# Latent attention: two heads at a time, block by block, with 64-row rotary score products

## The chip, the cores and the metric

One core of one Trainium2 chip runs the whole program. The metric is the device time of one execution in microseconds (us), taken as the median of several runs.

## The reference

Two transformer blocks, in 32-bit floats, on 512 tokens of width 1024. The first block has windowed attention, a short convolution and a mixture of 16 experts. The second block has two layers with feed-forward parts; its last mixer is the multi-head latent attention that the change touches. For each of its 8 heads:

```python
k = jnp.concatenate([k_nope, jnp.broadcast_to(k_pe[:, :, None, :], (B, S, N_HEADS_2, QK_ROPE))], axis=-1)
q = rope_tail(rmsnorm_2(q, q_head_norm), cos, sin)     # 128 plain dims + 64 rotary dims
k = rope_tail(rmsnorm_2(k, k_head_norm), cos, sin)
s = jnp.einsum('bhqd,bhkd->bhqk', q_blk, kt) * scale   # blocks of 128 queries
s = jnp.where(kpos[None, :] <= qpos[:, None], s, -jnp.inf)
p = jax.nn.softmax(s, axis=-1)
o = jnp.einsum('bhqk,bhkv->bhqv', p, vt)
```

So a score is a sum over 128 plain dimensions and 64 rotary ones, of which the rotary key is one for all heads before its scaling per head.

## The kernel before

All five engines run one hand-written program each; semaphores order them, and every engine works through its own list in order. SyncE (SP) loads weights through a ring of strips; ScalarE (ACT) and VectorE (DVE) split a strip into a high and a low part (helpers `hi` and `lo`), and TensorE (PE) makes three products of them (`three`, L1123 to L1125). This fills most of the time. The latent attention lies between the query projections and the output projection (`whole`, L1140).

**Layout.** `qn` and `kn` hold the 128 plain dimensions of queries and keys of each head on the 128 partitions. `qr` holds rotary queries, two heads to a tile: head 2i on partitions 0 to 63, head 2i+1 on 64 to 127. `kr` has one tile of 512 keys for each head; the scaled rotary key is written (`head_scale`, L2460) on that half of the partitions on which the head's queries lie. The other half is zero, from one memset on GpSimd (POOL) at L659, which waits until the memory is free (`h_lo` and `sq_done`); VectorE waits for it in front of the first `head_scale` (L2508).

**Units.** A unit u is one head h and one block b of 128 queries, h, b = divmod(u, 4): all four blocks of a head, then the next head. Being causal, block b has w = 128 (b + 1) keys. There are 32 units. For each, in this order:

- `scores(u)`, PE: a 32-bit product `qn` x `kn` (L1758), then one `qr` x `kr` over all 128 partitions (L1759), which adds to it, in one of four PSUM banks (`S2`, banks 6, 7, 1, 0). It counts up `scored`. For u >= 4 it waits until VectorE has taken unit u-4 out of the bank (`masked`).
- `soft_max(u)`, DVE: adds the causal mask and takes the maximum (L2536), and makes the bias (L2541).
- `soft(u)`, ACT: the exponential with its sum (L1087).
- `invert_sum`, `scale_probs`, DVE: reciprocal (L2032) and scaling (L2037) of unit u-1, behind `soft_max(u)` in VectorE's list.
- `turn_probs(u)`, PE: b + 1 transposes of 128x128 (L1780) into bank 2 or 3; it waits for the scaled probabilities and for ScalarE's copy of unit u-2 (`pt_act`).
- `turn_out(u)`, ACT: copies them into `pT2` (L1095).

When all four blocks of a head are turned, `values(h)`, PE, makes the value products (L1788); ScalarE (`head_out`, L1100) and VectorE (L2554) split the result into high and low parts.

**Order.** Turning runs three units behind the scores (LAG = 3). PE's list is

```python
for u in range(2, MH * NB + LAG + 1):
    if u < MH * NB:
        scores(u)
    if 0 <= u - LAG < MH * NB:
        turn_probs(u - LAG)
    if head_at(u - LAG - 1) is not None:
        values(head_at(u - LAG - 1))
```

where `head_at(u)` is the head whose last block is unit u, or None. ACT's list has `soft(u)`, then `turn_out(u - LAG)`, then `head_out` of the head that ended with unit u-LAG-2; DVE's list has `soft_max(u)`, then the reciprocal and scaling of unit u-1, then L2554 for the head that ended with unit u-LAG-3. One weight strip for the output projection is split meanwhile (`hi` at u = 8, `lo` at u = 11). The first two units' scores lie between the last four value projections (`values_of(1, i)`), whose results ScalarE copies out of banks 1, 3, 2 and 0 (`value_out`, L1036, semaphore `valued`); unit 2 goes into bank 1 and unit 3 into bank 0, so they wait for five and eight of these copies.

Of the kernel before, what the change touches and what calls it, by code (L numbers as in the profile page):

```python
# [28 lines left out]
P = 128  # L29
# [5 lines left out]
NB = T // P  # L35
# [5 lines left out]
MH, NOPE, ROPE = 8, 128, 64  # L41
# [85 lines left out]
def build(nc, A, out):  # L127
    st = ExitStack()
    with st:
# [113 lines left out]
        kr = place("kr", [P, MH, T], F32, G)  # L243
# [3 lines left out]
        qn = place("qn", [P, MH, T], F32, G + 50 * KB)  # L247
        qr = place("qr", [P, 4, T], F32, G + 66 * KB)
# [152 lines left out]
        def q_scale(h, b):  # L401

            c = 32 + 16 * (h // 4) + 4 * b + h % 4
            return qstat[:, c:c + 1]

        def head_at(u):

            return u // NB if 0 <= u < MH * NB and u % NB == NB - 1 else None

        def halves(n):  # L410

# [12 lines left out]
        S2 = (6, 7, 1, 0)  # L424
# [219 lines left out]
        @block.gpsimd  # L644
        def _(pool):
            pool.memset(ones[:, :], 1.0).then_inc(ones_set, 1)
            pool.memset(eps[:, :], EPS).then_inc(ones_set, 1)
            pool.wait_ge(mod_summed, 2)
            pool.memset(kZ[64:128, 0, :], 0.0).then_inc(cleared, 1)
            pool.memset(kZ[0:64, 1, :], 0.0).then_inc(cleared, 1)  # L650

            pool.wait_ge(strip_used, POOL)
            pool.memset(zero[:, :].bitcast(F32), 0.0).then_inc(cleared, 1)

            pool.wait_ge(select_loaded, 16)
            pool.tensor_copy(select_r[:, :, :], select[:, :, :]).then_inc(pool_made, 1)
            pool.wait_ge(h_lo, LO0[N2B])
            pool.wait_ge(sq_done, SQ0[N2B])
            pool.memset(kr[:, :, :], 0.0).then_inc(pool_made, 1)  # L659


        @block.scalar
        def _(act):
# [417 lines left out]


            def soft(u):
                h, b = divmod(u, NB)
                act.wait_ge(bias_ready, 32 + u + 1)
                p = prob2[:, u % 4, 0:(b + 1) * P]
                act.activation(p, p, ACT.Exp, bias=stat[:, 16 + u % 4:17 + u % 4], scale=q_scale(h, b),  # L1087
                               accum_out=stat[:, 20 + u % 4:21 + u % 4]).then_inc(exp_done, 1)

            def turn_out(u):  # L1090
                h, b = divmod(u, NB)
                act.wait_ge(p_turned, 32 + u + 1)
                if b == 0 and h >= 2:
                    act.wait_ge(pv_done, NB + h - 1)
                act.activation(pT2[h % 2][:, 0:b + 1, b * P:(b + 1) * P],  # L1095
                               pb[2 + u % 2][:, 0:(b + 1) * P].rearrange("p (k q) -> p k q", q=P), ACT.Copy).then_inc(pt_act, 1)
# [22 lines left out]
        def _(pe):  # L1119
# [625 lines left out]
                if s == 9:  # L1745
                    qsum_turn(0)
            def scores(u):
                h, b = divmod(u, NB)
                w = (b + 1) * P
                if u == 0:  # L1750
                    pe.wait_ge(out_taken, T_MOUT)
                    pe.wait_ge(hq_out, 2 * MH)
                    pe.wait_ge(rope_done, 10)
                if u in (2, 3):
                    pe.wait_ge(valued, 5 if u == 2 else 8)
                if u >= 4:
                    pe.wait_ge(masked, 32 + u - 3)
                pe.matmul(pb[S2[u % 4]][:, 0:w], qn[:, h, b * P:(b + 1) * P], kn[:, h, 0:w], start=True, stop=False)  # L1758
                pe.matmul(pb[S2[u % 4]][:, 0:w], qr[:, h // 2, b * P:(b + 1) * P], kr[:, h, 0:w], start=False, stop=True).then_inc(scored, 1)  # L1759

            head_sum(19)
            values_of(0, 0)
# [6 lines left out]
            values_of(1, 1)  # L1769
            scores(0)  # L1770
            values_of(1, 2)
            scores(1)
            values_of(1, 3)

            def turn_probs(u):
                h, b = divmod(u, NB)
                pe.wait_ge(p_ready, 32 + u + 1)
                pe.wait_ge(pt_act, 32 + u - 1)
                for k in range(b + 1):
                    mm = pe.transpose(pb[2 + u % 2][:, k * P:(k + 1) * P], prob2[:, u % 4, k * P:(k + 1) * P], tab("ident"))  # L1780
                mm.then_inc(p_turned, 1)

            def values(h):
                pe.wait_ge(pt_act, 32 + NB * h + NB)
                if h >= 2:
                    pe.wait_ge(att_lo, NB + h - 1)
                for k in range(NB):
                    mm = pe.matmul(pb[4 + h % 2][:, k * P:T], V2[:, k, h * P:(h + 1) * P], pT2[h % 2][:, k, k * P:T],  # L1788
                                   start=(k == 0), stop=(k == NB - 1))
                mm.then_inc(pv_done, 1)  # L1790

            for u in range(2, MH * NB + LAG + 1):
                if u < MH * NB:
                    scores(u)
                if 0 <= u - LAG < MH * NB:
                    turn_probs(u - LAG)
                if head_at(u - LAG - 1) is not None:
                    values(head_at(u - LAG - 1))
# [6 lines left out]
        def _(dve):  # L1805
# [228 lines left out]
            def scale_probs(v, p):  # L2034

                dve.wait_ge(inv_ready, v + 1)
                dve.tensor_scalar(p, p, stat[:, 24 + v % 4:25 + v % 4], None, ALU.mult).then_inc(p_ready, 1)  # L2037
# [451 lines left out]
            for s in range(12):  # L2489
                if s != 2:  # L2490
                    lo(M_Q + s + 2)
                dve.wait_ge(strip_used, M_Q + s + 1)
                ps = pb[bank(T_MQ + s)][:, :]
                if s in Q_ROPE:
                    dve.tensor_scalar(qr[:, Q_ROPE[s], :], ps, col("qh_rope"), None, ALU.mult).then_inc(out_taken, 1)
                else:
                    dve.tensor_copy(qn[:, Q_NOPE[s], :], ps).then_inc(out_taken, 1)
                if s == 2:
                    dve.wait_ge(hq_std, 1)
                    dve.reciprocal(head_rstd[:, :], head_std[:, :]).then_inc(hq_rstd, 1)  # L2500
                    dve.wait_ge(hq_rstd, 1)
                    dve.tensor_copy(head_hi[:, :], head_rstd[:, :]).then_inc(hq_rstd, 1)
                    dve.wait_ge(hq_rstd, 2)
                    dve.tensor_tensor(head_lo[:, :], head_rstd[:, :], head_hi[:, :], ALU.subtract).then_inc(hq_rstd, 1)
                    lo(M_Q + 4)
                if 3 <= s <= 6:
                    if s == 3:
                        dve.wait_ge(pool_made, 2)  # L2508
                        dve.wait_ge(gained, 2)
                        dve.wait_ge(keyed, 8)  # L2510
                        dve.wait_ge(rope_done, 6)
                    head_scale(2 * s - 6)
                    head_scale(2 * s - 5)
                if s == 7:
                    invert(NQL)
                if 8 <= s <= 11:
                    r = s - 7
                    rope_finish(qr[:, r - 1, :], pb[7 - r % 2][:, :], rope2[:, 1, :], rope2[:, 0, :], rope_tmp[:, :], 5 + r)
                if s == 10:
                    mean_squares(0)  # L2520
# [4 lines left out]


            def soft_max(u):
                h, b = divmod(u, NB)
                w = (b + 1) * P
                m2 = stat[:, 32 + u % 4:33 + u % 4]  # L2530
                dve.wait_ge(scored, 32 + u + 1)
                if u >= 4:
                    dve.wait_ge(p_turned, 32 + u - 3)
                else:
                    dve.wait_ge(mask_loaded, 16)
                dve.tensor_tensor_reduce(prob2[:, u % 4, 0:w], pb[S2[u % 4]][:, 0:w], cmask[:, T - w:T], 1.0, -3e38,  # L2536
                                         ALU.add, ALU.max, m2).then_inc(masked, 1)
                dve.wait_ge(masked, 32 + u + 1)
                if u in (0, 4 * NB):
                    dve.wait_ge(scale_ready, NB if u == 0 else 2 * NB)  # L2540
                dve.tensor_scalar(stat[:, 16 + u % 4:17 + u % 4], m2, q_scale(h, b), -1.0, ALU.mult, ALU.mult).then_inc(bias_ready, 1)  # L2541

            for u in range(MH * NB + LAG + 3):
                if u < MH * NB:
                    soft_max(u)
                if u == 11:
                    lo(M_OUT + 1)
                if 1 <= u <= MH * NB:
                    invert_sum(32 + u - 1)
                    scale_probs(32 + u - 1, prob2[:, (u - 1) % 4, 0:((u - 1) % NB + 1) * P])  # L2550
                if head_at(u - LAG - 3) is not None:
                    h = head_at(u - LAG - 3)
                    dve.wait_ge(att_hi, NB + h + 1)
                    dve.tensor_tensor(oL[:, h, :], pb[4 + h % 2][:, :], oH[:, h, :], ALU.subtract).then_inc(att_lo, 1)  # L2554
# [101 lines left out]
```

## Time and profile before

| what | value |
|---|---|
| median of 3 runs | 2512.27 us (2511.79 to 2514.25) |
| span of the profiled execution, first to last instruction | 2510.8 us |
| own time of that execution beyond its span | not shown; the median is 1.5 us above the span |
| PE busy, share of the span | 2478.2 us, 99% |
| DVE / ACT / POOL busy | 1155.5 / 742.0 / 8.0 us |
| L1759, rotary scores | 64 records, all between 2035 and 2096 us |
| mean granted clock of TensorE | 0.996 of full speed |

A product of 32-bit floats stands in the profile as two records, each with its own load of weights. A record of a matmul is longer than the time after which the next one can start, since it holds the way through the array as well, so starts are to be compared, not lengths; the chain of waits does that. Busy time of PE that comes from overlapping records is counted once.

### The profile page before, as it was taken

The numbers are of one execution on the slowest core, as the hardware profiler recorded it, in microseconds if no ns is written. First come the engines' busy times: TensorE is split into PE (matmuls) and PEld (weight loads), VectorE is DVE, ScalarE is ACT, GpSimd is POOL, SyncE is SP. The second block draws the span as 40 slices with busy tenths as digits, with TensorE's granted clock in tenths as the row PEclk, the third lists the DMA queues.
The fourth block names the chain that finished last, engine by engine and source line by source line (L and its number), as shares of the span: only waits on it lengthen the run. The fifth ranks groups of instructions, "written<-read, shape, count | busy, mean of one in ns | idle before, by whom it ended". The sixth has DMA issues, their size and how long they took to land.

```text
span 2510.8 us, 29196 instructions
## 1 busy us (share of the span) xinstructions
PE 2478.2 (99%) x10958; PEld 1783.1 (71%) x10958; DVE 1155.5 (46%) x1802; ACT 742.0 (30%) x1066; POOL 8.0 (0%) x11
## 2 busy tenths in 40 slices
PE   8999999999999999999999999999999999999999
PEld 4876733333336888888888888888887667888887
DVE  6785612222227544436444434444337665544422
ACT  4245210100114333224333223333224354333311
POOL 0000000000000000000000000000000000000000
PEclk9999999999999999999999999999999999999999
DMA  7530899999993323313232322233322211323332
GB/s 308 176 126 31 320 394 422 421 422 422 422 411 133 100 92 110 104 63 102 92 100 95 115 82 92 93 100 105 104 81 76 80 43 35 98 94 100 105 104 68
DMA packets 84644, 404.12 MB, mean 161 GB/s; under 512 B 9176, under 2 KB 9560, under 8 KB 60896
## 3 DMA queue, kind: packets, MB, share of 16 engines
q1 hardware_dynamic: 84576, 403.22, 43.7%
q8 instruction: 42, 0.69, 0.1%
q14 instruction: 26, 0.21, 0.0%
HBM read 401.08 MB, written 2.10 MB: 161 GB/s over the span
## 4 chain that ended last, share of the span: by engine, by line
PE 92%; DVE 3%; ACT 2%; issue 1%; DMA 1%; SPq 0%; ACTq 0%; DVEq 0%
PE pair L1123 23%; PE pair L1125 23%; PE pair L1124 23%; PE pair L1399 9%; PE pair L1424 4%; PE pair L1350 2%; PE pair L1650 1%; PE pair L1370 1%; PE pair L1788 1%; PE pair L1265 1%; PE pair L1758 1%; PE pair L1759 1%; PE pair L1371 1%; ACT wH L676 0%; DMA stage<-in_gate 0%
## 5 line engine op out<-in xcount | busy, mean ns | idle before, releaser
L1813 DVE TENSOR_TENSOR wL<-stage,wH 128x1024 fp32r<-128x1024 f32 (+3 forms) x301 | 388.9, 1292 | 771.1 <-ACT wH L676 770.7
L1123 PE MATMUL pair<-hH,wH 128*128 128x512 f32 x1672 | 658.4, 394 | 7.8 <-DVE hL L1858 2.4
L1125 PE MATMUL pair<-hH,wL 128*128 128x512 f32 x1672 | 652.0, 390 | 0.0
L1124 PE MATMUL pair<-hL,wH 128*128 128x512 f32 x1672 | 652.0, 390 | 0.0
L676 ACT ACTIVATE wH<-stage 128x1024 fp32r<-128x1024 f32 (+3 forms) x301 | 335.3, 1114 | 846.9 <-PE pair L1125 843.4
L1123 PEld LDWEIGHTS pair<-hH,wH 128*128 128x128 f32 x1672 | 314.6, 188 | 78.4 <-DVE hL L1858 4.1
L1124 PEld LDWEIGHTS pair<-hL,wH 128*128 128x128 f32 x1672 | 314.6, 188 | 67.1 <-issue 2.4
L1125 PEld LDWEIGHTS pair<-hH,wL 128*128 128x128 f32 x1672 | 314.6, 188 | 66.3
L1123 PE MATMUL pair<-gH,wH 128*128 128x512 f32 x704 | 273.9, 389 | 0.0
L1124 PE MATMUL pair<-gL,wH 128*128 128x512 f32 x704 | 273.9, 389 | 0.0
L1125 PE MATMUL pair<-gH,wL 128*128 128x512 f32 x704 | 273.9, 389 | 0.0
L1399 PE MATMUL pair<-ring,xsT 128*64 128x512 f32 x1008 | 223.9, 595 | 1.5 <-ACT xsT L903 1.5
L1399 PEld LDWEIGHTS pair<-ring,xsT 128*64 128x64 f32 x1008 | 71.2, 137 | 138.0 <-issue 136.3
L1124 PEld LDWEIGHTS pair<-gL,wH 128*128 128x128 f32 x704 | 132.1, 188 | 27.7
L1123 PEld LDWEIGHTS pair<-gH,wH 128*128 128x128 f32 x704 | 132.1, 188 | 27.5
L1125 PEld LDWEIGHTS pair<-gH,wL 128*128 128x128 f32 x704 | 132.1, 188 | 27.2
L2189 DVE SCALAR_TENSOR_TENSOR x<-pair,mod,x 128x512 f32<-128x512 f32 x64 | 45.5, 747 | 135.8 <-PE pair L1371 135.8
L716 ACT ACTIVATE sg<-hraw 128x512 f32<-128x512 f32 x88 | 55.7, 633 | 167.1 <-DVE hraw L2284 167.1
L1424 PE MATMUL pair<-ring,hidT 128*64 128x512 f32 x448 | 99.2, 595 | 0.0
L2293 DVE TENSOR_TENSOR gL<-gf,gH 128x512 f32 (+1 forms) x88 | 61.0, 693 | 78.7 <-ACT gH L719 78.7
L910 ACT ACTIVATE sil<-pair 128x512 f32<-128x512 f32 x16 | 8.7, 594 | 245.6 <-PE pair L1399 245.6
L719 ACT ACTIVATE gH<-gf 128x512 f32 (+1 forms) x88 | 55.7, 633 | 76.7 <-DVE gf L2290 76.7
(353 smaller groups left out, 2148.3 us busy)
## 6 DMA issues: line engine op xcount, KB each, us to landing
ring<-in_experts SPq DMA_DIRECT2D x182, 1024.0 KB, 21.0
stage<-in_gate SPq DMA_DIRECT2D x88, 512.0 KB, 3.6
stage<-in_up SPq DMA_DIRECT2D x88, 512.0 KB, 3.6
stage<-in_down SPq DMA_DIRECT2D x64, 704.0 KB, 4.0
adaw<-in_w_ada SPq DMA_DIRECT2D x32, 512.0 KB, 5.4
stage<-in_w_in SPq DMA_DIRECT2D x18, 512.0 KB, 3.9
ring<-in_experts SPq DMA_DIRECT2D x16, 512.0 KB, 11.6
stage<-in_mla_in SPq DMA_DIRECT2D x9, 512.0 KB, 3.6
```

Source lines behind the costliest of these rows:

```text
L676: act.activation(halves(n)[0], stage[:, n % STAGE, 0:width[n]], ACT.Copy).then_inc(strip_hi, 1)
L716: act.activation(sg[:, tile % 2, :], hraw[:, tile % 2, :], ACT.Silu).then_inc(silu_done, 1)
L719: act.activation(dst, gf[:, tile % 2, :], ACT.Copy).then_inc(g_hi, 1)
L1123: pe.matmul(ps, lh, rh, start=first, stop=False)
L1124: pe.matmul(ps, lh, rl, start=False, stop=False)
L1125: return pe.matmul(ps, ll, rh, start=False, stop=last)
L1350: mm = pe.matmul(pb[6 + half][:, :], pick[:, k, :], xt[:, k, half * 512:(half + 1) * 512], start=(k == 0), stop=(k == NB - 1))
L1399: mm = pe.matmul(pb[2 * g + half][64 * j:64 * j + 64, :], xsT[:, k, 64 * j:64 * j + 64], w[j][:, half * 512:(half + 1) * 512], start=(k == ...
L1424: mm = pe.matmul(pb[4 + half][64 * j:64 * j + 64, :], hidT[:, k, 64 * j:64 * j + 64], w[j][:, half * 512:(half + 1) * 512], start=(k == 0) ...
L1813: dve.tensor_tensor(low, stage[:, n % STAGE, 0:w], high, ALU.subtract).then_inc(strip_lo, 1)
L2189: dve.scalar_tensor_tensor(out=x[:, k, :], in0=pb[7 - k % 2][:, :], scalar=mod[:, 40 + k:41 + k], in1=x[:, k, :], op0=ALU.mult, op1=ALU.ad ...
L2293: dve.tensor_tensor(gL[:, g, :], gf[:, s, :], gH[:, g, :], ALU.subtract).then_inc(g_lo, 1)
```

## The change

- Units are renumbered: `head_block(u)` gives heads 2i and 2i+1 in turn, block by block: (head 0, block 0), (head 1, block 0), (head 0, block 1), and so on. `head_at` and all users of h and b follow, and so do the counts that `values` waits for.
- `scores(u)` runs for even u alone and makes both units: the two plain products, then the two rotary ones. The rotary product of head 2i reads partitions 0 to 63 of `qr` and `kr`, that of head 2i+1 partitions 64 to 127.
- It waits for `masked` of unit u-3 in place of u-4, and for u = 2 for all eight value copies. Unit 1's scores move to the place of unit 0's, ahead of the last two value projections.
- The memset of `kr` goes; VectorE waits for `h_lo` and `sq_done` itself.

```diff
+        def head_block(u):
+
+            two, rest = divmod(u, 2 * NB)
+            return 2 * two + rest % 2, rest // 2
+
         def head_at(u):
 
-            return u // NB if 0 <= u < MH * NB and u % NB == NB - 1 else None
+            return head_block(u)[0] if 0 <= u < MH * NB and head_block(u)[1] == NB - 1 else None
...
             pool.tensor_copy(select_r[:, :, :], select[:, :, :]).then_inc(pool_made, 1)
-            pool.wait_ge(h_lo, LO0[N2B])
-            pool.wait_ge(sq_done, SQ0[N2B])
-            pool.memset(kr[:, :, :], 0.0).then_inc(pool_made, 1)
...
             def soft(u):
-                h, b = divmod(u, NB)
+                h, b = head_block(u)
...
             def scores(u):
-                h, b = divmod(u, NB)
+
+                h, b = head_block(u)
                 w = (b + 1) * P
...
-                if u in (2, 3):
-                    pe.wait_ge(valued, 5 if u == 2 else 8)
+                if u == 2:
+                    pe.wait_ge(valued, 8)
                 if u >= 4:
-                    pe.wait_ge(masked, 32 + u - 3)
-                pe.matmul(pb[S2[u % 4]][:, 0:w], qn[:, h, b * P:(b + 1) * P], kn[:, h, 0:w], start=True, stop=False)
-                pe.matmul(pb[S2[u % 4]][:, 0:w], qr[:, h // 2, b * P:(b + 1) * P], kr[:, h, 0:w], start=False, stop=True).then_inc(scored, 1)
+                    pe.wait_ge(masked, 32 + u - 2)
+                for j in range(2):
+                    pe.matmul(pb[S2[(u + j) % 4]][:, 0:w], qn[:, h + j, b * P:(b + 1) * P], kn[:, h + j, 0:w], start=True, stop=False)
+                for j in range(2):
+                    rows = slice(64 * j, 64 * j + 64)
+                    pe.matmul(pb[S2[(u + j) % 4]][:, 0:w], qr[rows, h // 2, b * P:(b + 1) * P], kr[rows, h + j, 0:w],
+                              start=False, stop=True).then_inc(scored, 1)
...
             scores(0)
             values_of(1, 2)
-            scores(1)
             values_of(1, 3)
...
             def values(h):
-                pe.wait_ge(pt_act, 32 + NB * h + NB)
+                pe.wait_ge(pt_act, 32 + 2 * NB * (h // 2) + 2 * (NB - 1) + h % 2 + 1)
...
             for u in range(2, MH * NB + LAG + 1):
-                if u < MH * NB:
+                if u < MH * NB and u % 2 == 0:
                     scores(u)
...
                     if s == 3:
-                        dve.wait_ge(pool_made, 2)
+                        dve.wait_ge(h_lo, LO0[N2B])
+                        dve.wait_ge(sq_done, SQ0[N2B])
```

`turn_out`, `turn_probs`, `soft_max` and the scaling of unit u-1 take h and b from `head_block` in the same way. The lists of ACT and DVE keep their order by u.

## Rows read from the trace of the kernel before

**Rows 1.** Windows view, 2057 to 2103 us: length, busy time of each engine, PEclk, DMA.
```profile
core 0 of [0], span 2510.8 us
2057.00:2103.00 46.00, 45.05 (x196) 29.21 (x197) 28.96 (x112) 26.09 (x73) 0.00 (x0) 1.00 0.04 12
```

**Rows 2.** Chain of waits, one head's period: start us, length us, what.
```profile
2064.87 2.38 PE pair L1788 x8
...
2068.35 0.43 PE pair L1759 x2
2068.78 0.33 PE pair L1780 x3
...
2069.75 0.65 PE pair L1759 x2
...
2071.70 0.86 PE pair L1759 x2
...
2072.66 2.38 PE pair L1788 x8
```

**Rows 3.** Timeline of PE, first block's attention: start us, length us, what.
```profile
195.72 0.71 PE L1252 MATMUL pair<-tabs,prob 128*128 128x128 f32 x5
196.36 4.51 PE L1265 MATMUL pair<-PT,V 128*64 128x512 f32 x20
200.81 0.70 PE L1236 MATMUL pair<-kZ,qT 128*128 128x256 f32 x2
201.34 0.59 PE L1237 MATMUL pair<-kZ,qT 128*128 128x256 f32 x2
```

**Rows 4.** Timeline of PE, window means of the pool mixer, 1146.59 to 1148.58 us.
```profile
1146.59 0.49 PE L1590 MATMUL pair<-zero 1*128 1x512 f32 x1
1147.01 1.22 PE L1594 MATMUL pair<-band,tok 128*128 128x144 f32 x8
1148.16 0.49 PE L1590 MATMUL pair<-zero 1*128 1x512 f32 x1
```

**Rows 5.** Timeline of all engines behind a 512-key unit's scores, 2080.19 us on.
```profile
2080.19 0.27 PE L1780 MATMUL pair<-tabs,prob 128*128 128x128 f32 x1
2080.39 0.69 DVE L2536 CUSTOM_DVE_ANT_0 prob<-pair,cmask 128x512 f32<-128x512 f32 x1 [0.88 <-PE pair L1759]
...
2081.12 0.21 DVE L2541 TENSOR_SCALAR stat<-stat,qstat 128x1 f32<-128x1 f32 x1
...
2081.37 0.82 ACT L1087 ACTIVATE prob<-prob,stat,qstat 128x512 f32<-128x512 f32 x1 [1.01 <-DVE stat L2541]
...
2081.44 0.42 DVE L2037 TENSOR_SCALAR prob<-prob,stat 128x384 f32<-128x384 f32 x1
2082.09 0.18 ACT L1087 ACTIVATION_READ_ACCUMULATOR prob<-prob,stat,qstat 128x1 f32 x1
```

**Rows 6.** Groups by form, 2035 to 2103 us, ACT: busy us, mean ns, idle before.
```profile
L1095 ACT ACTIVATE pT2b<-pair 128x384 f32<-128x384 f32 x4 | 1.9, 484 | 0.0
...
L1036 ACT ACTIVATE V<-pair 128x512 f32<-128x512 f32 x3 | 1.8, 591 | 0.0
```

**Rows 7.** Timeline of PE at two of its waits, then the chain at the end.
```profile
2043.22 0.59 PE L1759 MATMUL pair<-kr,qr 128*128 128x256 f32 x2
2044.41 0.30 PE L1780 MATMUL pair<-tabs,prob 128*128 128x128 f32 x1 [0.59 <-ACT pT2a L1095]
...
2056.00 0.27 PE L1780 MATMUL pair<-tabs,prob 128*128 128x128 f32 x1
2057.03 0.70 PE L1788 MATMUL pair<-pT2b,V 128*128 128x512 f32 x1 [0.75 <-ACT pT2b L1095]
...
2096.05 2.38 PE pair L1788 x8
...
2100.53 2.42 PE pair L1788 x8
```

**Rows 8.** Source view of the memset of kr and of kr's first writer: durations, first start.
```profile
L659 POOL MEMSET kr<- x1: 3735/3735/3735, 1937.7 to 1937.7; 128x4096 f32 x1
...
L2460 DVE TENSOR_TENSOR kr<-krope,pair x8: 671/682/693, 1975.5 to 1996.2; 64x512 f32<-64x512 f32 x8
```

More of the change, by code:

```diff
@@ L1747, in scores @@
             def scores(u):
-                h, b = divmod(u, NB)
+                h, b = head_block(u)
                 w = (b + 1) * P
@@ L1771, in _ @@
             values_of(1, 2)
-            scores(1)
             values_of(1, 3)
             def turn_probs(u):
-                h, b = divmod(u, NB)
+                h, b = head_block(u)
                 pe.wait_ge(p_ready, 32 + u + 1)
@@ L2527, in soft_max @@
             def soft_max(u):
-                h, b = divmod(u, NB)
+                h, b = head_block(u)
                 w = (b + 1) * P
@@ L2549, in _ @@
                     invert_sum(32 + u - 1)
-                    scale_probs(32 + u - 1, prob2[:, (u - 1) % 4, 0:((u - 1) % NB + 1) * P])
+                    scale_probs(32 + u - 1, prob2[:, (u - 1) % 4, 0:(head_block(u - 1)[1] + 1) * P])
                 if head_at(u - LAG - 3) is not None:
```

## The prediction

> **What bounds the kernel now.** I read the granted clock and busy time of the stretch first. In the settled part of the latent attention, 2057 to 2103 us, the matmul side of TensorE is busy 45.05 of 46 us at full clock (PEclk 1.00, the 2.4 GHz level), and VectorE and ScalarE 29 and 26 us [rows 1]. So TensorE sets the pace and the others have idle time, on the average of the stretch. Then the chain of waits for one head, from one value product to the next: 2064.87 to 2072.66, 7.79 us [rows 2]. It is TensorE all the way: the score products without rotary (L1758), those with it (L1759), the turning of the probabilities (L1780), the value product (L1788). The two score products cost the same at each width, 0.43, 0.65 and 0.86 us for 256, 384 and 512 keys (0.22 for 128, a quarter of the last), though half of the partitions of the rotary one hold zeros. Below, S(u), T(u) and V(h) are the scores, the turning and the values of unit u and head h, C(u) ScalarE's copy of T(u), and w the width.
>
> **Term 1, the rotary products.** Per head L1759 takes 0.22 + 0.43 + 0.65 + 0.86 = 2.16 us [rows 2]. If the two products of a pair, on partitions 0 to 63 and 64 to 127, run at the same time, one of the two is free: 4 pairs x 2.13 (1280 columns, at 0.86 for 512) = 8.5 us saved. The trace has no pair on two halves of the rows. The nearest is a pair on two halves of the columns: 20 records of L1265, each 128x512, lie in 196.36 to 200.87 [rows 3]. One of those records streams for 0.43 us (half of the 0.86 of an L1759 product, which is two records, [rows 2]); 20 in a row would be 8.6 us, and they took 4.5, so two run at once, from the first pair on. I take the same for rows: bounds 0 us (no overlap) and 8.5 us, value 8.5.
>
> **Term 2, changing the shape of the array.** Each pair needs a 64-row product behind 128-row ones, and 128-row ones behind it: 16 times there and back. A product that uses one row among products that use 128 shows the price: from one L1590 to the next is 1.57 us [rows 4]. Its stream takes 0.21 us (512 columns at 2.4 GHz) and its eight followers 4 products of 144, 144, 144 and 128 columns, 560/512 x 0.86 = 0.94 us [rows 2], so 0.42 us are lost per there and back. The column shape says the same: the next product starts at 196.36 where five turnings of 0.11 from 195.72 would end at 196.27; it gives 10 x 0.43 = 4.30 of stream in the 4.45 us to 200.81; and then 0.53 instead of 0.43 to 201.34 [rows 3]: 0.09 + 0.15 + 0.10 = 0.34. I take 0.40, as the row shape is the nearer one: 16 x 0.40 = 6.4 us lost. Bounds: 0 (if rows change shape for free, which no row excludes) and 6.8. The Trainium skill, "TensorEngine Tiling (Array Packing)", Tiling Modes, says that changing the tiling mode drains the engine, without a price; by that rule the term stands, without it the sum would be 6.4 us of TensorE time lower. The trace agrees with the rule (0.34 and 0.42 us).
>
> So TensorE's own work falls by 8.5 - 6.4 = 2.1 us in all.
>
> **Term 3, the order of the units.** Here I expect the time to go. TensorE issues S(u, u+1), T(u-3), T(u-2), S(u+2, u+3), and both units with 512 keys become ready together. ScalarE is in order: exp(u) stands ahead of C(u-3). T(v) waits for C(v-2). V(h) of both heads comes two units later, so the pair of long softmaxes is no longer covered by a value product of 2.38 us, as each one is now.
>
> The chain of one 512-key unit [rows 5]: TensorE's last stream ends at 2080.19; 0.20 later the maximum starts; exp starts 0.98 after that (2081.37) and ends with its accumulator at 2082.27, 0.90 long. VectorE is free for the next unit's maximum 1.41 us after the first began (2081.44 + 0.42 less about 0.06 of pipelining; the same scale of 384 keys follows in the new order). So, from the end of S(14, 15): exp(15) starts at 0.20 + 1.41 + 0.98 = 2.6 and ends at 3.5; behind it stands C(12), 0.48 [rows 6]; with 0.1 for its hand-over T(14) can start at 4.1. TensorE's own work up to there is T(11) 0.22, T(12) 0.33, S(16, 17) of 128 keys 0.64 + 0.40, T(13) 0.33 (0.11 each 128 keys) = 1.92. The new idle time is 4.1 - 1.9 = 2.2 us, part of it ahead of T(13), which waits for C(11) behind exp(14), the rest ahead of T(14). It comes behind units 6-7, 14-15 and 22-23: 2.2 x 3 = 6.6. Behind 30-31 there is no S to fill: 4.1 - 0.9 = 3.2, and about 0.4 ahead of V(6) = 3.6.
>
> The start: S(2, 3) now waits for the last of the eight value copies, since it writes the bank that frees last: 0.20 + 0.59 for the copy [rows 6] = 0.85 with the hand-over; before, the wait stood only ahead of S(3) and S(2) covered it. Sum of idle time after: 6.6 + 3.6 + 0.85 = 11.0 us.
>
> Idle time before, which the new order does not keep [rows 7]: T(2) starts at 2044.41, 0.76 after the end of the S(5) stream (2043.22 + 0.43); V(1) at 2057.03, 0.92 after T(6) (2056.00 + 0.11); at the end, between V(6) (ends 2098.43 on the chain, which counts the tail) and V(7) (2100.53) lie 2.10 us, of which T(30) and T(31) take 0.87: 1.2, or 1.3 with the tail; and six times about 0.12 ahead of a V: 0.7. Sum 3.7. The new idle time is 11.0 - 3.7 = 7.3 us.
>
> **Edits at nothing.** The memset of kr ran on GpSimd from 1937.7, 3.7 us, and its result is first wanted at 1975.5 [rows 8]: 34 us early, so its removal gives 0. VectorE now waits for the two semaphores that the memset waited for; both were up when it began at 1937.7, so these cost 0 too. Were that cover gone it would cost 3.7 us. The rewritten counts and indices change no work. Nothing on SP's queue moves; the stage moved 12 GB/s [rows 1].
>
> **The sum.** -8.5 + 6.4 + 7.3 = +5.2 us. The profiled span is 2510.8 us [rows 1], so 2516.0 after; the median of the runs shown is 2512.27, 1.5 above the span (the profiled execution's own time beyond its span is not shown), which I take to stay: 2517.5 us, +0.21%. I count 0.2%, 5.0 us, as what a measurement of this kernel can tell from no change, so the forecast sits just past that edge.
>
> **Rivals.**
> 1. *Cheap shape changes.* With 0 us in term 2 most of the gain falls into idle time, since the work that fills the gaps shrinks with it: S(14, 15) and S(16, 17) both lie inside the chains above, of exp(13) and C(10) ahead of T(12) and of exp(15) and C(12) ahead of T(14), so of the 1.6 us of a pair's four changes about 1.0 goes to waiting. Following the three engines' orders through with the same durations I get 4.2 of the 6.4 us lost so: -8.5 + 7.3 + 4.2 = +3.0, 2515.3 us, which is the same. At half the price +4.1, 2516.4, the same too. For: no row shows 64-row products. Against: both neighbours paid. This is my case on the other side, not slower: it decides where a there and back costs under about 0.36 us.
> 2. *No overlap of the row halves.* Then term 1 is 0, and the gaps shrink a little as S takes longer: +8.1, 2520.4 us, slower. For: a single fp32 product is two records, and if the four of a pair stream in program order only the middle two overlap: 3 slots for 4, +6.2, 2518.5. Against: the column pairs overlap from the first pair on [rows 3]. The Trainium skill, "TensorE: Matmul & The Clock Gate", Part 3, says that matmuls in distinct row groups run concurrently; by it term 1 is 8.5 us, by no overlap it is 0, and no row of the trace shows it for rows.
> 3. *The softmax keeps up.* If VectorE and ScalarE have the two long units done in time, the 7.3 us vanish and the time falls by 2.1 to 2510.2 us, with free shape changes as well to 2503.8. For: each is idle for over a third of the stretch [rows 1]. Against: it is the latency of the in-order chain, not their share, and it is read from rows that hold it whole [rows 5].
> 4. *The clock falls* in gaps of 1.8 us. Against: PEclk is 1.00 in a stretch that includes waits of 0.9 to 1.2 us [rows 1, 7]. I give it nothing of its own.
>
> **Chances.** Forecast, +4.5 to +6: 0.40, cut by the edge of 5.0 us into 0.30 above and 0.10 below. Cheaper shape changes, +3 to +4.5: 0.30. Little or no overlap, +6 to +8.5: 0.18. The softmax keeps up: 0.12, of which 0.04 at -2.1 (the same) and 0.08 with cheap shape changes besides (faster). Slower 0.30 + 0.18 = 0.48, same 0.10 + 0.30 + 0.04 = 0.44, faster 0.08. The range goes from 2512.0, no change, which leaves out the 0.12 of a softmax that wholly keeps up, to 2520.6, no overlap.
>
> **What would show it.** Starts of L1759 in pairs a few ns apart, 32 pairs of records; about 0.1 us ahead of and behind each; new waits of PE on C (L1095) of 0.6 to 1.9 us in front of L1780, four clusters some 17 us apart (two heads: 2 x 7.79 + 1.35); two value products almost back to back; the stage from the first L1758 to the first L1123 behind the last V 5 us longer. Wrong in term 3 if PE's waits in the stage sum to under 7 us; in term 1 if the starts of L1759 are one after another.

## The result, and the profile after

The changed kernel takes 2521.43 us (median of 10 runs, 2517.73 to 2525.27), the kernel before, run again beside it, 2513.19 (10 runs, the three of the table above among them, 2509.56 to 2515.36): ratio 1.0033, 95% interval 1.0024 to 1.0041. It is 8.2 us slower; I had forecast 5.2 and a time of 2517.5. The measured time lies 0.8 us above my range.

The windows view of the changed kernel shows the stage as [rows 1] did before (length, busy time of PE, PEld, DVE, ACT, POOL, PEclk, DMA share, GB/s):

```profile
2057.00:2103.00 46.00, 40.10 (x178) 22.23 (x176) 27.77 (x110) 24.90 (x70) 0.00 (x0) 0.99 0.04 12
```

TensorE is busy 40 us where it was 45. Its waits in the stage, first of the changed kernel, then of the kernel before (us in total, times, longest):

```profile
PE pair L1786 <- ACT pT2a L1097: 4.4, 7, 1.0
PE pair L1786 <- ACT pT2b L1097: 3.7, 4, 1.6
PE pair L1762 <- ACT V L1038: 0.7, 1, 0.7
```
```profile
PE pair L1788 <- ACT pT2b L1095: 1.4, 2, 0.8
PE pair L1780 <- ACT pT2a L1095: 0.6, 1, 0.6
PE pair L1780 <- ACT pT2b L1095: 0.2, 1, 0.2
```

8.8 us in place of 2.2, all but 0.7 of it the turning (L1786) behind ScalarE's copies (L1097): the named step on the named releaser. This view counts a wait from the end of a record, which includes the way through the array. Counted as the prediction did, from the end of a stream to the next start, TensorE's waits in the same trace sum to 11.2 us where I had 11.0, and 3.7 before, as I had.

The timeline of PE of the changed kernel, from the plain products of a 512-key pair on (start, length, what), answers to [rows 3] and [rows 4]:

```profile
2063.74 1.02 PE L1762 MATMUL pair<-kn,qn 128*128 128x512 f32 x2
2064.69 1.13 PE L1765 MATMUL pair<-kr,qr 64*128 64x512 f32 x4
2065.75 0.44 PE L1786 MATMUL pair<-tabs,prob 128*128 128x128 f32 x2
2066.43 0.52 PE L1786 MATMUL pair<-tabs,prob 128*128 128x128 f32 x3 [0.24 <-ACT pT2a L1097]
...
2068.52 0.52 PE L1786 MATMUL pair<-tabs,prob 128*128 128x128 f32 x3 [0.69 <-ACT pT2b L1097]
2070.01 0.41 PE L1786 MATMUL pair<-tabs,prob 128*128 128x128 f32 x2 [0.97 <-ACT pT2a L1097]
```

Three things can be read. The four records of the two 64-row products take 1.13 us with the tail, 1.06 from start to start of the next line; in a row they would be 4 x 0.43 = 1.72. The halves of the rows do overlap; two products of a pair start 6 to 7 ns apart. The change of shape costs 0.09 ahead (two plain records from 2063.74 end at 2064.60), 1.06 - 0.86 = 0.20 within and at the way out, and about 0.06 between the first two turnings behind it (0.17 us from start to start, where 0.11 is usual), 0.35 in all. And the turnings T(12), T(13) and T(14) each start late, 0.4, 0.9 and 1.1 us after the stream ahead of them ended (0.1 of the 0.9 is the way out of the 64-row shape).

VectorE shows one thing that I had left out. When the streams of S(14, 15) end, at 2065.75, it is busy with the low part of a head's result (L2561), so the maximum of unit 14 starts 0.47 us later and not 0.20:

```profile
2065.62 0.68 DVE L2561 TENSOR_TENSOR nL<-pair,nH 128x512 fp32r<-128x512 f32 x1
2066.22 0.68 DVE L2543 CUSTOM_DVE_ANT_0 prob<-pair,cmask 128x512 f32<-128x512 f32 x1
```

T(14) starts 4.26 us after those streams, where the prediction had 4.1.

Of the 8.2 us, the stage has 6.7: from the start of the first plain score record to that of the last value record it was 2034.93 to 2102.68 = 67.75 us before and is 2036.88 to 2111.35 = 74.47. The other 1.5 us lie outside it. What I had not counted within it is at its end. The windows of the changed kernel there:

```profile
2099.00:2101.00 2.00, 1.15 (x7) 0.51 (x5) 1.93 (x7) 1.09 (x4) 0.00 (x0) 1.00 0.00 0
2101.00:2103.00 2.00, 0.77 (x3) 0.40 (x3) 1.55 (x7) 1.79 (x6) 0.00 (x0) 0.77 0.00 0
2103.00:2109.00 6.00, 5.54 (x14) 3.60 (x15) 0.62 (x2) 1.89 (x4) 0.00 (x0) 0.51 0.00 0
2109.00:2111.00 2.00, 2.00 (x9) 1.23 (x8) 0.69 (x1) 0.60 (x1) 0.00 (x0) 1.00 0.00 0
```

TensorE works 1.92 of 4 us behind the last pair of 512-key units, the granted clock falls to 0.5, the 1.2 GHz level, and comes back to 1.00 near 2109. The first of the two last value products lies in that spell (timeline of PE):

```profile
2101.97 0.77 PE L1786 MATMUL pair<-tabs,prob 128*128 128x128 f32 x3 [1.56 <-ACT pT2b L1097]
2103.45 1.94 PE L1786 MATMUL pair<-tabs,prob 128*128 128x128 f32 x8 [0.72 <-ACT pT2a L1097]
2105.23 4.24 PE L1794 MATMUL pair<-pT2a,V 128*128 128x512 f32 x8
2109.30 1.02 PE L1794 MATMUL pair<-pT2b,V 128*128 128x512 f32 x2
```

From 2105.23 to 2109.30 it takes 4.07 us from start to start, where a value product of the kernel before took 2.26 (2080.42 to 2082.68).

### The profile page after: what moved, and what is told of

The parts are those of the page before. It is cut to its first block, busy times and chain, and to the rows that moved or that the text cites. A ratio compares the mean times of both kernels' runs of the same rounds, so it can differ in the third digit from the quotient of the medians.

```text
span 2519.4 us, 29195 instructions
## 1 busy us (share of the span) xinstructions
PE 2479.4 (98%) x10958; PEld 1779.5 (71%) x10958; DVE 1151.5 (46%) x1802; ACT 742.4 (29%) x1066; POOL 4.2 (0%) x10
## 4 chain that ended last, share of the span: by engine, by line
PE 91%; DVE 4%; ACT 2%; issue 1%; DMA 1%; DVEq 0%; ACTq 0%
PE pair L1125 23%; PE pair L1126 22%; PE pair L1127 22%; PE pair L1401 9%; PE pair L1426 4%; PE pair L1352 2%; PE pair L1652 1%; PE pair L1794 1%; PE pair L1372 1%; PE pair L1267 1%; PE pair L1373 1%; DMA stage<-in_gate 0%; PE pair L1762 0%; ACT wH L678 0%; PE pair L1254 0%
```

## The experiments

Theory A is the prediction's sum (waits of the softmax chain, shape changes, overlap) with the fall of the clock added. Rivals: B, the excess is from outside the stage or the clock has nothing to do with the gap; C, the shape changes cost the time, not the order; D, VectorE, not ScalarE's order, sets the gaps. The medians are of runs beside the kernel before on the same chip. "Stage" is the length defined above.

| kernel | ratio to before, 95% | stage us | clock at 0.5 in the stage |
|---|---|---|---|
| before | 1 | 67.75 | no |
| changed | 1.0033 (1.0024 to 1.0041) | 74.47 | at the end |
| changed, again | 1.0034 (1.0022 to 1.0045) | 74.49 | at the end |
| order only | 1.0020 (1.0011 to 1.0029) | 71.63 | no |
| 64 rows only | 1.0037 (1.0024 to 1.0051) | 75.79 | no |
| changed, end filled | 1.0021 (1.0011 to 1.0031) | 73.61 | early, not at the end |
| changed, all gaps filled | 1.0018 (1.0009 to 1.0027) | 72.20 | no |
| changed, copy first | 1.0012 (1.0003 to 1.0021) | 70.47 | at the end |
| before, copy first | 0.9992 (0.9983 to 1.0001) | 64.76 | no |
| three buffers, copy first | 0.9985 (0.9976 to 0.9994) | 63.29 | no |
| the same again | 0.9979 (0.9970 to 0.9988) | 63.28 | no |
| three buffers alone | 0.9994 (0.9985 to 1.0003) | 67.38 | early |

**The changed kernel again.** No edit.

> The changed kernel once more, for its time beside the kernel before on one chip and for a second profile. Theory A (the time goes into waits of the softmax chain at the 512-key units, 11 us in place of 3.7, into sixteen shape changes of about 0.36 us, and into a spell of half clock behind the last gap, about 2.3 us, against 8.5 us saved by the overlap): 6 to 9 us slower, the stage from the first plain score product to the last value product 72.5 us without a fall of the clock and 74.5 with one, against 67.8 before. Rival B (the part beyond 5.2 us comes from outside the stage, where the first profile of the changed kernel was already 2 us late at 2035 us): the stage starts 2 us late again; by A that was chance and the start moves by up to 2 us either way.

Measured: 2520.62 us against 2513.91, 6.7 slower; the stage began at 2033.43, earlier than in the kernel before's profile, and took 74.49 us. So the late start of the first profile was chance, and rival B falls. The clock fell at the same place again:

```profile
2098.00:2106.00 8.00, 6.72 (x20) 4.40 (x21) 1.71 (x7) 3.22 (x9) 0.00 (x0) 0.57 0.00 0
```

**The order alone.**

```diff
-                    rows = slice(64 * j, 64 * j + 64)
+                    rows = slice(0, P)
```

with the memset of `kr` and VectorE's wait for it put back.

> The changed order (two heads block by block, both units' scores issued together), but with the rotary products over all 128 partitions and the zeros in place, as before. No work is saved and no shape changes. Theory A: idle time of TensorE in the stage rises from 3.7 to about 8.2 us, so +4.5 us, 72.3 us for the stage, and about 1 us more where the clock falls at the end. Rival C (the shape changes, not the order, cost the time): no change.

Measured: 4.2 us slower (2518.06 against 2513.91), stage +3.9. With no 64-row product in it the new order alone costs about what I said (4.5). Rival C falls. The clock stayed at 1.00, so the extra us for a fall was not due, although this kernel is as sparse at its end as the changed one:

```profile
2097.20:2101.20 4.00, 1.77 (x14) 1.19 (x12) 2.38 (x8) 3.36 (x9) 0.00 (x0) 1.00 0.00 0
```

**64 rows alone.** In the kernel before:

```diff
-                pe.matmul(pb[S2[u % 4]][:, 0:w], qr[:, h // 2, b * P:(b + 1) * P], kr[:, h, 0:w], ...
+                rows = slice(64 * (h % 2), 64 * (h % 2) + 64)
+                pe.matmul(pb[S2[u % 4]][:, 0:w], qr[rows, h // 2, b * P:(b + 1) * P], kr[rows, h, 0:w], ...
```

> The kernel before in its old order, each rotary product on its own 64 partitions, one after another, none next to another of the other half. No overlap is possible; every unit changes the shape there and back. Theory A: 32 changes of 0.36 us, less a little where one falls into a wait: +10 to +11.5 us, and the product itself takes as long on 64 rows as on 128. Rival (shape changes are cheap between rows of 128 and 64): under +3 us.

Measured: 8.5 us slower (2522.38), stage +8.0, less than the 10 to 11.5 I had said. The timeline of PE of this kernel at two heads' first units:

```profile
2072.18 0.39 PE L1758 MATMUL pair<-kn,qn 128*128 128x128 f32 x2
...
2081.13 0.39 PE L1758 MATMUL pair<-kn,qn 128*128 128x128 f32 x2
```

A head takes 8.95 us where it took 7.79 [rows 2]: 1.16 for four changes, 0.29 each net, since a wait of 0.12 ahead of V and part of V's own start are swallowed; at the start and the end of the stage longer waits swallow more. I had allowed too little for that. Within one unit the change is as dear as in the pair:

```profile
2076.80 1.02 PE L1758 MATMUL pair<-kn,qn 128*128 128x512 f32 x2
2077.76 1.12 PE L1760 MATMUL pair<-kr,qr 64*128 64x512 f32 x2
2078.81 0.33 PE L1781 MATMUL pair<-tabs,prob 128*128 128x128 f32 x1
```

2077.76 to 2078.81 is 1.05 us for two records of 64 rows that stream for 0.86, and 0.10 lie ahead. A product on half the rows alone is as long as on all of them. The same 1.06 us held four records in the pair.

**The gaps filled.** Products that nobody reads, put into idle time: at the end alone,

```diff
+                if u - LAG in (MH * NB - 3, MH * NB - 2):
+                    pe.wait_ge(masked, 32 + MH * NB - 3)
+                    for k in range(2 if u - LAG == MH * NB - 3 else 1):
+                        pe.matmul(pb[6][:, :], qn[:, 0, 0:P], kn[:, 0, :], start=True, stop=True)
```

> The changed kernel with three products of 128x512 that nobody reads, in the two gaps at the end (two ahead of the turning of unit 29, one ahead of unit 30, 0.86 us each). They lie in idle time of 1.8 and 1.2 us. Theory A: the granted clock stays at 1.00 to the end of the stage, the last turnings and the first value product run at 0.11 and 2.26 us again in place of 0.21 and 4.08, so 2 us faster than the changed kernel where that has its fall. Rival B (the fall has nothing to do with the gap): the clock falls as before, the time is the same or longer by the fillers.

and in all the gaps behind 512-key units (there into bank 1, of 384 and 512 columns):

> The changed kernel with products that nobody reads in all of its gaps: behind each pair of 512-key units one of 128x384 ahead of the turning of the first 384-key unit's neighbour and one of 128x512 ahead of the next, at the end two and one of 128x512. All lie in idle time (0.76 and 1.2 us; 1.8 and 1.2 at the end). Theory A: no fall of the clock anywhere in the stage, which takes 72 to 72.8 us; 2 us faster than the changed kernel. Rival B: the clock falls in the stage all the same.

Measured: with the end filled the clock is at 1.00 there (third row below), but it fell behind the first gap of the stage (second row). The edit touches nothing there, and in neither profile of the changed kernel had it fallen at that place. The stage is 73.6 us, the median 2518.55.

```profile
2039.00:2112.00 73.00, 66.07 (x287) 37.31 (x286) 41.38 (x171) 40.74 (x109) 0.00 (x0) 0.98 0.05 15
2055.00:2059.00 4.00, 4.00 (x15) 2.61 (x16) 1.19 (x7) 2.54 (x7) 0.00 (x0) 0.57 0.02 4
2100.00:2112.00 12.00, 11.39 (x43) 5.70 (x42) 6.96 (x23) 7.03 (x17) 0.00 (x0) 1.00 0.00 0
```

With all gaps filled it fell nowhere in the stage:

```profile
2034.00:2107.00 73.00, 70.80 (x307) 39.30 (x306) 42.03 (x174) 41.48 (x111) 0.00 (x0) 1.00 0.04 15
```

The stage is 72.20 us: adding work to TensorE took 2.3 us off it. Both fillings show where. From the start of the last pair's rotary products, T(30) starts after 5.32 us in all four profiles, filled or not, so the fillers delay nothing and shorten no wait. From there to the last value record it is 7.90 and 7.92 us in the changed kernel and 5.62 in both filled ones. So 2.3 us is the price of the fall at the end, 74.48 - 72.20, and 72.20 - 67.75 = 4.45 us is what the rest of the change costs. An early fall, as with the end alone filled, costs 1.4 us (73.61 - 72.20). The median went from 6.7 to 3.6 us above the kernel before, though the intervals of the two ratios overlap (1.0022 to 1.0045 and 1.0009 to 1.0027), so the profiles, not the medians, carry this.

What makes the clock fall is shown in part only. It fell at the unfilled end in each of the three profiles of kernels with 64-row pairs that leave it open (the changed one twice and the one of the next experiment), and at neither filled end. But it did not fall at the end of the kernel with the order alone (1.77 us of work in 4), nor behind the settled gaps of the changed kernel, which are nearly as sparse:

```profile
2066.00:2070.00 4.00, 2.10 (x16) 1.44 (x15) 3.79 (x16) 2.88 (x9) 0.00 (x0) 1.00 0.00 0
```

Behind the first gap it fell with the end filled and not in the changed kernel, though the two are the same up to there. So filling the waits keeps the clock up; which unfilled wait brings a fall stays open.

**ScalarE's copy ahead of the exponential.** In ScalarE's loop, in the changed kernel and in the kernel before:

```diff
+                if 0 <= u - LAG < MH * NB:
+                    turn_out(u - LAG)
                 if u < MH * NB:
                     soft(u)
-                if 0 <= u - LAG < MH * NB:
-                    turn_out(u - LAG)
```

> The changed kernel with ScalarE's two steps swapped in its loop: the copy of unit u-3's turned probabilities ahead of the exponential of unit u. Theory A (the turning waits for a copy that stands behind the exponential of a 512-key unit): TensorE's waits fall by about 3 us, the stage to 69.5 us without a fall of the clock (72.2 for the changed kernel), so 3 us faster, a little more where the fall behind the last gap goes with it. Rival D (VectorE's part of the chain, maximum and scaling, sets the gaps, not ScalarE's order): under 1 us.

> The same swap in the kernel before. Its waits that hang on a copy behind an exponential: ahead of T(2), ahead of V(1), at the end, and 0.12 ahead of each other V. Theory A: 2.4 us less, the stage 65.4 us (67.8 before). Rival D: no change.

Measured: the changed kernel is now 2.4 us above the kernel before where it was 6.7 above. Its stage of 70.47 us has one fall of the clock, to 0.72 on the mean of 2099 to 2105, so it is 1 us above the 69.5 named; that the fall accounts for this is an estimate. Its waits of PE:

```profile
PE pair L1786 <- DVE prob L2043: 6.0, 8, 1.2
PE pair L1762 <- ACT V L1038: 0.7, 1, 0.7
```

The copy is gone from the list, and what is late next is VectorE's scaling, with 6.0 us. So both are right: up to the last pair's rotary products, where the clock is at 1.00 in both kernels, the stage takes 58.57 us in place of 61.26, so the order of ScalarE cost 2.7 us, and under it rival D's chain holds the rest. In the kernel before the swap gave 2.2 us by the medians, with an interval that just includes no change, and 3.0 in the stage (67.75 to 64.76), where I had said 2.4.

**Three buffers.** A version that keeps the overlap and covers the gaps. `kr` gives two heads one tile, since each needs half of the rows; the freed 8 KB a partition become a third `pT2`, and the value product of an odd head waits for the next pair's gap:

```diff
-        kr = place("kr", [P, MH, T], F32, G)
+        kr = place("kr", [P, MH // 2, T], F32, G)
...
+                if u - LAG >= 8 and (u - LAG) % 8 == 0:
+                    values((u - LAG) // 4 - 2)
+                if u - LAG >= 13 and (u - LAG) % 8 == 5:
+                    values((u - LAG - 13) // 4 + 1)
                 if 0 <= u - LAG < MH * NB:
                     turn_probs(u - LAG)
-                if head_at(u - LAG - 1) is not None:
-                    values(head_at(u - LAG - 1))
+            values(MH - 1)
```

with ScalarE's copy ahead of the exponential, and `head_out` and VectorE's low part moved accordingly.

> A version meant to keep the overlap and lose the gaps: the changed kernel with kr packed into four tiles (two heads share one), the freed 8 KB a partition as a third buffer of turned probabilities, so that the value product of each odd head can wait until unit 8i+13 and lie in the gap behind the next pair's 512-key units; ScalarE's copy ahead of the exponential, as in the swap. Theory A: waits of TensorE fall from 11 to about 2.7 us, the stage to 63.5 to 64 us against 67.8 before: 4 us faster than the kernel before and 8 faster than the changed one, with the clock at 1.00. Rival D or an unknown wait: the gaps move instead, the stage over 66 us.

> The version with three buffers and the swap once more, beside the one without the swap on the same chip: 4 to 6 us faster than the kernel before again, the stage 63.3 us, no fall of the clock in it.

Measured: 2508.16 against 2513.11 us and 2508.76 against 2514.78, 5 and 6 us faster than the kernel before. Each against its own kernel before, that is 12 to 14 us better than the changed one, where I had said 8; the stage, at 63.29 and 63.28, is 11.2 shorter. Its timeline of PE shows the long products of a 512-key pair and, behind the next pair's short scores, a value product in the place of the gap:

```profile
2055.42 1.88 PE L1765 MATMUL pair<-kn,qn 128*128 128x512 f32 x4
2057.23 1.13 PE L1768 MATMUL pair<-kr,qr 64*128 64x512 f32 x4
2058.29 0.76 PE L1789 MATMUL pair<-tabs,prob 128*128 128x128 f32 x5
2058.89 0.61 PE L1765 MATMUL pair<-kn,qn 128*128 128x128 f32 x4
2059.43 0.49 PE L1768 MATMUL pair<-kr,qr 64*128 64x128 f32 x4
2059.86 2.42 PE L1797 MATMUL pair<-pT2b,V 128*128 128x512 f32 x8
2062.11 0.93 PE L1789 MATMUL pair<-tabs,prob 128*128 128x128 f32 x7
```

Its waits of PE are 2.0 us:

```profile
PE pair L1789 <- DVE prob L2049: 1.3, 2, 0.9
PE pair L1765 <- ACT V L1038: 0.7, 1, 0.7
```

Without the swap in ScalarE's list:

> The version with packed kr, a third buffer and the odd heads' value products in the gaps, but with ScalarE's old order, exponential ahead of copy. It tells what the moved value products are worth by themselves. Theory A: waits of TensorE about 4.9 us, the stage 65.5 to 66 us (63.3 with the swap, 67.8 for the kernel before, 72.2 for the changed one): 2 us faster than the kernel before. Rival D (the swap of ScalarE's steps does the work, the moved products little): the stage near 69 us.

Measured: 2513.0 against 2514.78 us; the stage 67.38 with a spell of half clock early in it, so above the 65.5 to 66 named. The spell lies behind the first gap, at the same place as in the kernel with its end filled, where it cost 1.4 us; by that estimate the stage is 66.0 us without it. The moved products and the swap each bring part of the gain.

## Why the prediction was wrong

Point by point:

- **Term 1, the rotary products.** Right: 8.5 us by overlap, from the first pair on. Pairs run at once; a single product gains nothing. The four records of a pair take two slots, not the three of rival 2. This agrees with the Trainium skill, "TensorE: Matmul & The Clock Gate", Part 3, by which matmuls in distinct row groups run concurrently.
- **Term 2, shape changes.** Taken 0.40 each from a one-row product, measured 0.35 (0.355 before rounding): 5.7 in place of 6.4 us. Right in kind. The Trainium skill's drain at a change of tiling mode ("TensorEngine Tiling (Array Packing)", Tiling Modes) agrees with this. Rival 1, cheap changes, falls with the 8.0 us of stage that the kernel with 64 rows alone lost.
- **Term 3, the order.** Right in mechanism and place, T(12) to T(14) behind C behind exp, 2.4 us a settled boundary where I had 2.2; at the end 3.2 us of waits ahead of the turnings, as I had. One reading of the kernel before had a slip: between V(6) and V(7) lie T(29), T(30) and T(31), nine turnings of 0.98 us and not 0.87, and the waits there are two, 0.40 and 0.85 us; their sum, about 1.3, came out right all the same. By itself the order costs 3.9 us of stage. The 64-row pairs on top of it, 2.8 us less work, brought nothing: 72.20 us without a fall against 71.63. The softmax chain sets the length of the gaps, so what TensorE saved turned into waits, as rival 1 had said of cheap changes. I named ScalarE's list; the swap shows that VectorE's scaling stands close behind it.
- **The sum of the three.** Forecast +5.2, measured +4.45 in the kernel without a fall of the clock, and that kernel ran 3.6 us above the kernel before. The mechanism was right and its size 0.8 too high.
- **Rival 4, the clock.** This is the step that failed. I wrote that PEclk is 1.00 in a stretch that includes waits of 0.9 to 1.2 us, and gave the rival nothing. That was no evidence for the new kernel: the wait of 0.92 us ends at 2057.03, ahead of the stretch read, and the 1.2 us are the two waits of 0.40 and 0.85. The end of the changed stage has T(28), T(29) and T(30) each behind a wait, 0.4, 1.7 and 1.0 us, 1.92 us of work in 4, and there the clock fell to 0.5 in both profiles, which is worth 2.3 us. With the 4.45 that makes 6.7 us of stage; without the fall the time would lie within my range. My own sum had the long idle time at the end in it (3.2 us); I did not ask what TensorE's clock would do there.
- **The base.** 2512.27 was the median of three runs; with more, the kernel before has 2513.11 to 2514.78. So about 0.9 us of the 3.9 between 2517.5 and 2521.43 was there beforehand, and 2.3 are the clock. The sum was 0.8 too high, so 1.5 us are left, the part outside the stage. No run explains them; the interval of the ratio reaches from 6.0 to 10.3 us, and in the repeat the whole difference, 6.7 us, is that of the stage. The time passed the end of the range by 0.8 us, less than each of the three parts, so that it did so at all was a matter of chance; that the stage lost 2.3 us more than its three terms was not.

## What to carry to other kernels

Before two units are issued together, write down what covered the latency of each one; here the value product between two long softmaxes covered more (7.3 us of new waits) than the pairing saved (8.5 us of stream, less 5.7 for changing the array's shape). The memory that a change frees may buy the cover back, as the packed keys did. And where a forecast adds idle time to TensorE, give the clock a price and a chance of its own: a gap costs its length, and where the clock falls, the work behind it at half speed as well.

## What the runs showed that I had not expected

- A kernel with more work on TensorE is faster: three useless products at the end and two in each gap took the stage from 74.5 to 72.2 us.
- Ahead of the stage the twelve kernels do the same work on TensorE, yet the stage starts between 2032 and 2039 us. Windows of the changed kernel and of the kernel before,

```profile
764.00:774.00 10.00, 7.46 (x26) 5.99 (x27) 7.07 (x11) 3.60 (x6) 0.00 (x0) 0.83 0.35 109
```
```profile
764.00:774.00 10.00, 7.87 (x34) 6.45 (x35) 8.25 (x12) 5.02 (x8) 0.00 (x0) 1.00 0.33 109
```

  show a spell at half clock in one and none in the other, with no edit between them that touches this place. Seven of the twelve profiles have it. Their stages start at 2032.7 to 2038.8 us, those of the other five at 2032.1 to 2036.3, so the spell can be part of the spread at most; the rest was not looked into. A gain of a few us is best read from the stage's own length.
